# A transformer trunk on one core: gate and up tiles as twins, with Strassen-type block products in 8 of 11 FFN tiles a layer

## What is computed

```python
D_MODEL, SEQ, DEPTH = 2048, 256, 2
FFN_HIDDEN = ((-(-8 * D_MODEL // 3)) + 255) // 256 * 256      # 5632

def swiglu(xn, w_gate, w_up, w_down):
    return (jax.nn.silu(xn @ w_gate) * (xn @ w_up)) @ w_down
...
        x = x + swiglu(rms_norm(x, ffn_norm[layer]), w_gate[layer], w_up[layer], w_down[layer])
```

## Time and profile before

| | us |
|---|---|
| median of 3 runs | 2103.17 (2102.14 to 2103.26) |
| the profiled execution | 2102.08 |
| its span, first to last instruction | 2100.5 |
| TensorE busy | 2094.3 |
| VectorE busy | 1454.3 |
| ScalarE busy | 1017.5 |

### The profile page before, as it was taken

One profiled execution on the slowest core, in us unless ns is written; L12 is line 12 of the kernel. 1 busy time (PEld: TensorE's weight loads), 2 busy tenths in 40 slices (PEclk: granted clock), 3 DMA queues, 4 the chain that ended last, 5 costly groups with the idle time before them and its releaser, 6 DMA issues.

```text
span 2100.5 us, 27240 instructions
## 1 busy us (share of the span) xinstructions
PE 2094.3 (100%) x9288; PEld 1733.0 (83%) x9288; DVE 1454.3 (69%) x2019; ACT 1017.5 (48%) x1276; POOL 77.7 (4%) x85
## 2 busy tenths in 40 slices
PE   9999999999999999999999999999999999999999
PEld 7888888888888888888888888888888888888887
DVE  5777677666667666565576776586676667669887
ACT  6555455444444444444455566554444444445453
POOL 0100011000000000000011000010000000000000
PEclk9999999999999999999999999999999999999999
DMA  8788666666666665556677774666666666666664
GB/s 279 227 267 255 200 211 203 182 189 208 191 194 185 190 201 182 190 188 205 196 231 240 240 220 151 204 198 197 182 190 205 194 191 184 189 203 202 216 205 151
DMA packets 235128, 427.22 MB, mean 203 GB/s; under 512 B 16048, under 2 KB 37680, under 8 KB 235056
## 3 DMA queue, kind: packets, MB, share of 16 engines
q1 hardware_dynamic: 232608, 422.07, 64.6%
q10 hardware_dynamic: 2448, 4.21, 0.5%
HBM read 410.23 MB, written 15.99 MB: 203 GB/s over the span
## 4 chain that ended last, share of the span: by engine, by line
PE 99%; DMA 0%; ACT 0%; DVE 0%; issue 0%; SPq 0%
PE psum L673 28%; PE psum L676 28%; PE psum L674 28%; PE psum L810 4%; PE psum L812 4%; PE psum L811 4%; PE psum L741 1%; PE psum L727 1%; PE psum L693 1%; PE psum L746 0%; DMA x_res<-in_x 0%; PE psum L762 0%; ACT w_hi L887 0%; ACT kt_a L1087 0%; DVE xt_lo L1259 0%
## 5 line engine op out<-in xcount | busy, mean ns | idle before, releaser
L1245 DVE TENSOR_TENSOR w_lo<-w_raw,w_hi 128x1024 fp32r<-128x1024 f32 x740 | 890.9, 1210 | 521.7 <-ACT w_hi L887 516.1
L887 ACT ACTIVATE w_hi<-w_raw 128x1024 fp32r<-128x1024 f32 x740 | 772.4, 1049 | 890.4 <-PE psum L676 752.5
L673 PE MATMUL psum<-w_hi,xt_hi 128*128 128x512 f32 x2012 | 790.8, 393 | 0.0
L676 PE MATMUL psum<-w_hi,xt_lo 128*128 128x512 f32 x2012 | 783.4, 389 | 0.0
L674 PE MATMUL psum<-w_lo,xt_hi 128*128 128x512 f32 x2012 | 783.0, 389 | 0.0
L676 PEld LDWEIGHTS psum<-w_hi,xt_lo 128*128 128x128 f32 x2012 | 377.7, 188 | 79.3
L674 PEld LDWEIGHTS psum<-w_lo,xt_hi 128*128 128x128 f32 x2012 | 377.8, 188 | 78.2
L673 PEld LDWEIGHTS psum<-w_hi,xt_hi 128*128 128x128 f32 x2012 | 377.8, 188 | 77.9
L673 PE MATMUL psum<-w_hi,ht_hi 128*128 128x512 f32 x608 | 240.6, 396 | 0.0
L676 PE MATMUL psum<-w_hi,ht_lo 128*128 128x512 f32 x608 | 236.9, 390 | 0.0
L674 PE MATMUL psum<-w_lo,ht_hi 128*128 128x512 f32 x608 | 236.6, 389 | 0.0
(11 more groups left out here) (171 smaller groups left out, 1006.2 us busy)
## 6 DMA issues: line engine op xcount, KB each, us to landing
w_raw<-in_w_gate SPq DMA_DIRECT2D x176, 512.0 KB, 3.8
w_raw<-in_w_up SPq DMA_DIRECT2D x176, 512.0 KB, 3.8
w_raw<-in_w_down SPq DMA_DIRECT2D x168, 512.0 KB, 4.4
w_raw<-in_cd_w_in SPq DMA_DIRECT2D x80, 512.0 KB, 4.5
w_raw<-in_ab_w_in SPq DMA_DIRECT2D x71, 512.0 KB, 4.7
w_raw<-in_ab_w_out SPq DMA_DIRECT2D x32, 512.0 KB, 4.3
w_raw<-in_cd_w_out SPq DMA_DIRECT2D x32, 512.0 KB, 3.7
block_dram<-turn_sb SPq DMA_DIRECT2D x18, 512.0 KB, 4.3
```

The lines of the kernel that those rows point to most:

```text
L673: nc.tensor.matmul(acc, hi[:, chunk, ts], w_hi[:, slot, c, :], start=first and c == 0, stop=False)
L676: mm = nc.tensor.matmul(acc, lo[:, chunk, ts], w_hi[:, slot, c, :], start=False, stop=end)
L887: nc.scalar.activation(w_hi[:, slot, 0:n, :], w_raw[:, slot, 0:n, :], ACT.Copy).then_inc(hi_ready, 1)
L1245: nc.vector.tensor_tensor(w_lo[:, slot, 0:n, :], w_raw[:, slot, 0:n, :], w_hi[:, slot, 0:n, :].bitcast(F32), ALU.subtract).then_inc(lo_rea ...
```

## The change

**The twins.** Units of gate and up now alternate: `UP_UNITS` is (gate, p), (up, p) for the chunk pairs p = 0 to 5, then gate 6, 7 and up 6, 7. A gate tile and the up tile of the same columns are thus the two tiles of a 2x2 block product. In the tiles 1 to 8 of each layer (`UP_FIRST` to `UP_LAST`) the pairs p = 2 and p = 5 (`UP_SEVEN`), units 4, 5 and 10, 11 of the tile, are done with seven products; tile 0 and tiles 9 and 10 are plain. The row sums depend on the layer's input alone: they are made once a layer, during tile 0. Weight sums are made in each tile, into space that is free meanwhile (`stages`, `probs`, the last eight chunks of `ht_*`).

**The ends.** After the second pair ScalarE copies the first bank and VectorE makes four sums (`up_combine`), into `stages` 2 and 3. When the plain products are complete too, VectorE adds them (`gate_sums`, `up_sums`), in the next tile's first units; Silu and the hidden product then read SBUF. Consecutive tiles use the two halves of PSUM in turn, so the loop holds two tiles.

**The turn.** The hidden tile is turned as the mixer's are: one transpose of the whole tile on VectorE (`blocks`, after unit 2 of the next tile), a write to DRAM that SyncE issues before load 9, and four reads before load 11. `hidden_hi` and `hidden_lo` are four instructions of 128x256 each, at units 11 and 12. The last tile of a layer is finished this way during the first units of the down product. The down product itself keeps its pairs; the order inside them is slightly rearranged, because its functions are now shared.

```diff
+UP_PLAIN_END = 6
+UP_UNITS = [(j, p) for p in range(UP_PLAIN_END) for j in range(2)]
+UP_UNITS += [(j, p) for j in range(2) for p in range(UP_PLAIN_END, UP_PAIRS)]
...
+UP_SEVEN = (2, 5)
+UP_FIRST, UP_LAST = 1, HT - 3
+BLOCKS_AT, BACK_AT, SPLIT_AT = 9, 11, 12
...
+            def move_hidden(layer, i, v):
+
+                if v == BLOCKS_AT:
+                    sp.wait_ge(blocks_ready, up_move(layer, i) + 1)
+                    sp.wait_ge(landed, up_move(layer, i) * 64)
+                    sp.dma_start(block_dram[:], turn_sb[:]).then_inc(blocks_out, 16)
+                if v == BACK_AT:
+                    sp.wait_ge(blocks_out, up_move(layer, i) * 16 + 16)
+                    for b in range(4):
+                        rows = block_dram[:, b].rearrange("(a j) x -> j a x", a=4)
+                        sp.dma_start(turn_sb[32 * b:32 * b + 32], rows).then_inc(landed, 16)
...
+                def up_tile(i, first=False):
+                    for idx, (j, p) in enumerate(UP_UNITS):
+                        if not first:
+                            move_hidden(layer, i - 1, idx)
+                        load(up_unit(layer, i, idx), idx % RING, (w_gate, w_up)[j][layer], UC * p, UC, bass.ds(i * N, N))
...
+                    pe.wait_ge(lo_ready, u + 1)
+                    own(only_bank(odd, 0), rows, p, 0, 0, w_hi[:, a, 0, :], w_lo[:, a, 0, :], first, last)
+                    mm = own(bank_of(odd, 0, 0), rows, p, 1, 0, w_hi[:, a, 1, :], w_lo[:, a, 1, :], False)
                     mm.then_inc(unit_used, 1)
+                    pe.wait_ge(lo_ready, u + 2)
+                    pe.wait_ge(s_ready, rows_done)
+                    mm = three(bank_of(odd, 1, 0), s_hi_of[:, 3, :], s_lo_of[:, 3, :], w_hi[:, b, 1, :], w_lo[:, b, 1, :],
+                               False)
                     mm.then_inc(unit_used, 1)
+                    pe.wait_ge(tl_ready, s * 2 + 4)
+                    for k, t, which in ((0, 0, 1), (2, 1, 3), (1, 2, 2)):
+                        three(only_bank(odd, which), s_hi_of[:, k, :], s_lo_of[:, k, :], t_hi_of[:, t, :], t_lo_of[:, t, :],
+                              first, last)
+                    own(bank_of(odd, 0, 1), rows, p, 1, 1, t_hi_of[:, 3, :], t_lo_of[:, 3, :],
+                        False).then_inc(seven_used, 1)
...
+            def finish_up(layer, i, odd, twin, idx):
+
+                if twin and idx == 0:
+                    gate_sums(layer, i, odd)
+                if twin and idx == 2:
+                    up_sums(layer, i, odd)
+                if idx == 3:
+                    hidden(layer, i, odd, twin)
+                if idx == SPLIT_AT:
+                    hidden_lo(layer, i)
...
+            def up_tile(layer, i, odd, twin, before, first=False):
+
+                for idx, (j, p) in enumerate(UP_UNITS):
+                    u = up_unit(layer, i, idx)
...
+                    if not first:
+                        finish_up(layer, i - 1, not odd, before, idx)
+                    if twin and p in UP_SEVEN and j == 1:
+                        sum_lows(up_sum(layer, i, UP_SEVEN.index(p)), UP_T)
+                        split_lower(u, idx % RING)
+                    else:
+                        split(u, idx % RING)
...
+                    if twin and j == 1 and p + 1 in UP_SEVEN:
...
+                        weight_sums(u + 1, (idx + 1) % RING, up_sum(layer, i, UP_SEVEN.index(p + 1)), UP_T)
+                    if twin and idx == 2 * UP_SEVEN[-1] + 1 + LEAD:
+                        up_combine(layer, i, odd)
```

More of the change, by code:

```diff
@@ L484, in turn_count @@
         def turn_count(layer, name, n):
-            return n + (ph[name, layer]["th"] - 2 * XT) // 2 + 1 - 2 * (layer + 1)
+            return n + 1 + {("out", 0): -2, ("down", 0): 2, ("out", 1): 4}[name, layer]
         def split_count(layer, name, half):
@@ L634, in _ @@
                          slice(n * N, n * N + N))
[L635 to L639, removed]
+                def up_tile(i, first=False):
[3 more added lines that the diff above has]
+                        load(up_unit(layer, i, idx), idx % RING, (w_gate, w_up)[j][layer], UC * p, UC, bass.ds(i * N, N))
+                up_tile(0, True)
+                with sp.Fori(0, HT - 1) as i:
+                    up_tile(i + 1)
                 if layer == 1:
@@ L794, in _ @@
                         attention(layer, KU * len(m.tiles) + i)
[L796 to L806, removed]
                 def three(acc, a_hi, a_lo, b_hi, b_lo, start, stop=False):
@@ new lines, in own, with seven_products @@
+                    return three(acc, rows[0][:, UC * p + c, ts], rows[1][:, UC * p + c, ts], b_hi, b_lo, start, stop)
+                def seven_products(odd, u, slot, rows, p, sums, lows, s, rows_done, first, last):
+                    a, b = slot, (slot + 1) % RING
+                    t_hi_of, t_lo_of = sums[1], sums[2]
+                    s_hi_of, s_lo_of = lows
+                    pe.wait_ge(lo_ready, u + 1)
+                    own(only_bank(odd, 0), rows, p, 0, 0, w_hi[:, a, 0, :], w_lo[:, a, 0, :], first, last)
+                    mm = own(bank_of(odd, 0, 0), rows, p, 1, 0, w_hi[:, a, 1, :], w_lo[:, a, 1, :], False)
@@ L1003, in hidden_hi @@
-            def hidden_hi(layer, i):
-                act.wait_ge(turned, turn_count(layer, "up", i))
-                for half in range(2):
-                    nc.scalar.activation(ht_hi[:, bass.ds(i * 4 + 2 * half, 2), :], turn_sb[:, 2 * half:2 * half + 2, :],
-                                         ACT.Copy).then_inc(t_hi, 1)
+                    if not twin:
+                        tok_done(0, tok, i + (pu["a"] + 1), up_unit(layer, i, UP_END[0] + 1))
+                    src = stage[2][:, tok, :] if twin else bank_of(odd, 0, tok)
@@ new lines, in silu @@
+                    ins = nc.scalar.activation(stage[2][:, tok, :], src, ACT.Silu, scale=rstd[:, 2 * layer + 1, tok:tok + 1])
+                    if not twin:
+                        ins.then_inc(acc_free[0], 1)
+                if twin:
+                    ins.then_inc(silu_ready, 1)
+            def hidden_hi(layer, i):
+                act.wait_ge(landed, up_move(layer, i) * 64 + 64)
+                for c in range(4):
+                    dst = ht_hi[:, bass.ds(i * 4 + c, 1), :].rearrange("p c t -> p (c t)")
+                    ins = nc.scalar.activation(dst.rearrange("p (t a i) -> p t a i", t=TOK, a=4), turned_chunk(c), ACT.Copy)
+                    if c % 2:
+                        ins.then_inc(t_hi, 1)
@@ new lines, in gate_sums, with up_sums @@
+                    nc.vector.tensor_tensor(stage[2][:, tok, :], bank_of(odd, 0, tok), stage[2][:, tok, :],
+                                            ALU.add).then_inc(acc_free[0], 1)
+            def up_sums(layer, i, odd):
+                pu = ph["up", layer]
+                for tok in range(TOK):
+                    tok_done(1, tok, i + (pu["b"] + 1), up_unit(layer, i, UP_END[1] + 1))
+                    nc.vector.tensor_tensor(stage[3][:, tok, :], bank_of(odd, 1, tok), stage[3][:, tok, :],
+                                            ALU.add).then_inc(acc_free[1], 1)
```

483 lines of the change are left out of this document (300 added, 183 removed).

## The result

The changed kernel takes **2126.82 us** (median of 4 runs, 2123.84 to 2128.07) against 2103.22 for the kernel before on the same chip: ratio 1.0111, 95% interval 1.0094 to 1.0129. It is slower by 23.6 us, where 2095 was forecast, and it lies outside the range of 2085 to 2112. The profiled execution took 2123.84 us.

What follows compares the result with a forecast made beforehand. TensorE's product count was taken as the bound: 21.7 us of products saved less 13.6 us of waits (14 tiles at 0.97) gave 8.1 us, 2094.0 profiled, 2095 us median with 1.1 added; range 2085 to 2112.

Steps and rivals of the forecast that it cites:

- The products: Gate/up block pairs on TensorE: 96 products fewer at 0.2265 us each, 21.7 us saved.
- VectorE's prices and its load: Steady twin tile: VectorE's operations, priced from the trace, sum to 36.6 us of the tile's 42.1, load 87%.
- no wait at the tile's end: After the second pair: combination ends near 36.6 us, its banks wanted at 43.1, so no wait.
- ScalarE covered: ScalarE gains two roundings of sums a pair and four smaller copies; busy 48% of the span, so it is covered.
- the first pair: First block pair of a steady tile: operands ready at 12.55 us, wanted at 12.23, wait 0.49 us with restart.
- the second wait: Second block pair of a steady tile: wait 0.48 us; landings up to 21.3 free, later ones cost their whole lateness.
- the landing of load 11: Last weight load before the second pair: lands at 10.2 + 4.8 + 1.8 + 5.0 = 21.8 us, bounds 20.3 to 23.5.
- rival 2: Turn's write and reads ahead of load 11 in SyncE's queue delay weights: landing 23.5, 37.4 us lost, 2119; chance 0.25.
- free by half a microsecond: Layer 1 down product, first pair: operands ready at 33.5 us, wanted at 34.0, so no wait.
- the first twin tiles: First twin tile of each layer: no additions ahead and its chain starts 2.5 us earlier, so no wait at either pair.

Runs made afterwards that it cites:

- no_moves: The change with the gate/up turn's write and four reads left out, semaphores still raised: 2092.67 us, ratio 0.9951.
- write_early: The change with the turn's write placed before load 8 in SyncE's queue instead of before load 9: 2125.53 us, ratio 1.0113.
- write_only: The change with only the four reads of each gate/up turn left out, the write and its wait kept: 2094.51 us, ratio 0.9957.

## Why the prediction was wrong

**Right.** The products (21.7 us), VectorE's prices and its load (36.4 us busy in the tile above, 36.6 counted), no wait at the tile's end, ScalarE covered, the first pair: 0.49 forecast, 0.66 measured in no_moves. And the form of the second wait: free up to a landing at 21.3, its whole lateness after. The table gives that point again. The change waits 2.77 - 0.66 = 2.11 us at the second pair with a landing at 23.45, write_early 1.80 with 23.15; both put it at 21.3.

**Wrong.** The step that failed is the landing of load 11, 10.2 + 4.8 + 1.8 + 5.0 = 21.8. The mean is 23.5. Term by term it was 10.6 + 5.0 + 1.9 + 6.0: the load leaves 0.7 us later than the sum has it, at 17.5, and the last term, its time in flight, is 6.0 us and not 5.0. I chose 5.0 between two rows, one read as nothing else in flight (4.1) and one as a single load in flight (6.0). Neither was so clean: in both the four reads were in flight too, and another load left 0.5 us behind. The one behind the row of 6.0 took 6.8 us, a slower row that I did not look at; the two in one view, with the median:

```profile
w_raw<-in_ab_w_out SPq DMA_DIRECT2D x2, 512.0 KB, 6.4
```

In the change two loads and four reads were in flight when load 11 left, and load 12 followed 0.7 us behind: the right end to take was the upper one. The room between 21.8 and 23.45 costs 14 x 1.65 = 23 us, most of the 29.8 by which the profiled execution missed 2094.0. This is rival 2, at its price: load 11 at 23.5 was to give 2119, and what lies above that is the first wait and what follows here.

**Missing from the sum.** The rest, 4.4 us: the down product (1.8), "free by half a microsecond" in the sum and longer in every kernel with the new code; the first twin tiles (1.9 in all), said to have no wait at either pair; 0.6 before gate/up, which is no more than two profiles of the kernel before differ by there (0.8). With the measured landing (14 x 2.11) and first wait (14 x 0.66) the sum is 2102.1 - 21.7 + 29.5 + 9.2 + 4.4 = 2123.5; the profiled execution took 2123.84. My range ended at a landing of 23.0 and had no room for these. The profiled execution was the fastest of the four, which spread over 4.2 us, so that the median lies 3.0 us above it and not 1.1; the kernel before spread over 1.4.

**What I did not ask.** I took the queue's order from the code and the latencies from rows, but never asked how full the DMA engines are in that stretch. From the sizes and the prediction's own times: loads 8 to 11, the write and the reads are 6 x 512 KB = 3.15 MB between 9.7 and 21.8 us, 260 GB/s, and with load 12, which leaves right behind, 303. The changed kernel moved 320 GB/s at a share of 0.99. The sum asked for nearly all that the engines gave, with latencies from stretches that I never checked for it. (By their shapes the weights are 390 MB in all, not the 422 MB given at the start.)

The Trainium skill's figure ("DMA: Bandwidth & Descriptors", Anatomy of one DMA) would, as an estimate, have had load 11 there at 19.2. The Trainium skill gives it per DMA and for those that GpSimd issues; here SyncE issued several at once, and the trace was 4.3 us away.

A rule of the Trainium skill that I did not weigh bears on the reads: "SBUF — State Buffer", Door 1: The DMA port swizzle, says that a transfer to 32 partitions reaches only 8 of 16 ports. The runs agree in direction. In the same 5.5 us of a tile, from 14.8 us behind its first matmul, the engines' share was 0.98 to 1.01 in four kernels. With the reads ahead of load 11 they moved 296 GB/s (the change) and 282 (write_early); without reads 339 (no_moves) and 358 (write_only). The change, then write_only:

```profile
606.60:612.10 5.50, 5.50 (x26) 4.57 (x25) 2.67 (x3) 2.08 (x3) 0.00 (x0) 1.00 0.98 296
598.81:604.31 5.50, 5.50 (x26) 4.56 (x25) 2.66 (x3) 2.31 (x3) 0.00 (x0) 1.00 1.01 358
```

No run here had the reads in another shape, so that the ports are the reason is not shown. A read also moves pieces of 1 KB where a load's are 2 KB, and that was not tested either.

## What to carry to other kernels

Where an engine waits in order for a whole load before a long chain, that load's landing is the deadline of everything ahead of it in the queue: put other transfers behind it, not ahead, and the work that feeds them later. Before taking a latency from a row, add up the bytes that will be in flight in that stretch; a mean DMA share of 0.68 hid one of 0.99. And an edit that costs nothing alone (the turn, 0 us in gate/up) and one that saves (the pairs) can lose together, here 23.6 us, by where they meet in one queue.

## What the hardware showed that I had not expected

- A load of 512 KB took 3.6 us (mean of load 6 of a tile) where nothing else was in flight, and 5.7 to 7.3 us (loads 10 to 13 of the change and of write_early) in a bunch; in the bunch it hardly mattered when it left (write_early: 1.0 us earlier out, 0.3 us earlier in).
- The loads of arrays with 2048 columns (output and down weights) are a little slower in every kernel with the new code. The fastest of the 32 loads of the output weights in layer 1 landed after 3.37 to 3.39 us in the three profiles of the old order and after 3.52 to 3.71 in all others, whose order in that stage is the old one; those of the gate weights show no such step (3.41 to 3.50 throughout). The reason was not found.
